# An early load of x, paired scores, and one tile's routing ahead of the other tile's work in a fused eight-mixer kernel

## The reference, cut to what matters

```python
# layer 0: differential attention, 8 heads of 2 maps (16 score maps of head size 64), v of 128
s = einsum('bhmqd,bhmkd->bhmqk', rope(q), rope(k)) * scale       # chunk mask: 64-token chunks
p = softmax(where(mask, s, -inf));  a = p[:, :, 0] - lam * p[:, :, 1]
o = rms_norm(a @ v) * subln_g * (1 - lambda_init)
x = layer_norm(ALPHA * x + o @ w_o)
# PEER, after each attention: 8 heads, 128 keys a side, 16 of 16384 experts a head
scores = einsum('thcd,hckd->thck', (x @ w_pq), sub_keys)
s_top, i_top = top_k(scores, 16)
g_s, g_i = top_k(all 16 x 16 sums of the two sides, 16);  gates = softmax(g_s)
h = gelu(einsum('td,ted->te', x, u[ids]))
ffn = einsum('te,ted->td', gates * h, v[ids])
x = layer_norm(ALPHA * x + ffn)
# layer 1: stick-breaking attention, then PEER again
```

## Time and profile before

| | us |
|---|---|
| median of 3 runs (3049.17 to 3051.73) | 3051.18 |
| the profiled execution | 3059.78 |
| its span, first to last instruction | 3058.1 |
| PE busy (share of the span) | 2584.2 (85%) |
| DVE busy | 1706.0 (56%) |
| ACT busy | 917.5 (30%) |
| POOL busy | 623.6 (20%) |
| mean granted PE clock | 0.961 of 2.4 GHz |

### The profile page before, as it was taken

One profiled execution on the slowest core, in us unless ns is written; L12 is line 12 of the kernel. 1 busy time (PEld: TensorE's weight loads), 2 busy tenths in 40 slices (PEclk: granted clock), 3 DMA queues, 4 the chain that ended last, 5 costly groups with the idle time before them and its releaser, 6 DMA issues.

```text
span 3058.1 us, 29977 instructions
## 1 busy us (share of the span) xinstructions
PE 2584.2 (85%) x10337; PEld 1604.8 (52%) x10337; DVE 1706.0 (56%) x3830; ACT 917.5 (30%) x1906; POOL 623.6 (20%) x623
## 2 busy tenths in 40 slices
PE   7997777777779887777777788999899989998999
PEld 3564222222237562222222245897579767975798
DVE  2336767767641256676776545554455465545654
ACT  1312222222213322222222124442444344423443
POOL 0003444444420023444444302000100000001000
PEclk9888999999999999999999999999999989998999
DMA  7208999999984169999999931553355324543353
GB/s 251 83 21 356 421 421 421 386 422 421 421 329 151 55 233 417 422 421 422 388 421 421 422 133 60 167 190 110 110 165 185 119 83 147 185 147 110 107 183 109
DMA packets 209663, 767.50 MB, mean 251 GB/s; under 512 B 16435, under 2 KB 87686, under 8 KB 143750
## 3 DMA queue, kind: packets, MB, share of 16 engines
q0 software_dynamic: 73760, 536.93, 42.4%
q1 hardware_dynamic: 135782, 229.09, 22.2%
HBM read 764.90 MB, written 1.07 MB: 250 GB/s over the span
## 4 chain that ended last, share of the span: by engine, by line
PE 40%; DMA 6%; DVE 3%; ACT 1%; issue 1%; POOL 0%; DVEq 0%; ACTq 0%; POOLq 0%
PE psum L1161 12%; PE psum L1175 11%; PE psum L917 9%; DMA weights<-in_peer_uv,scratch 4%; PE psum L1123 2%; DMA arena<-in_peer_uv,scratch 2%; PE psum L976 1%; PE psum L904 1%; PE psum L965 1%; PE psum L954 1%; PE psum L950 0%; DVE heads_arena L1939 0%; PE psum L1139 0%; DVE arena L1848 0%; DVE xT L2030 0%
## 5 line engine op out<-in xcount | busy, mean ns | idle before, releaser
L1123 PE MATMUL psum<-weights,scratch 128*128 128x512 f32 x1224 | 576.3, 616 | 202.8 <-ACT scratch L1494 202.8
L1123 PEld LDWEIGHTS psum<-weights,scratch 128*128 128x128 f32 x1224 | 226.0, 193 | 551.8 <-ACT scratch L1494 306.3
L1123 PE MATMUL psum<-arena,scratch 128*128 128x512 f32 x824 | 390.7, 619 | 143.8 <-ACT scratch L1494 143.8
L2333 POOL DMA_INDIRECT weights<-in_peer_uv,scratch x306 | 335.4, 1096 | 643.3 <-PE psum L1123 406.8
L917 PE MATMUL psum<-weights,xT 128*128 128x512 f32 (+2 forms) x1000 | 437.8, 596 | 19.7 <-ACT xT L1337 14.7
L2145 DVE TENSOR_TENSOR piece<-weights,piece 128x2048 fp32r<-128x2048 f32 x128 | 292.8, 2293 | 221.1 <-ACT piece L1535 221.1
L1161 PE MATMUL psum<-split_x,piece 128*128 128x256 f32 x3072 | 386.0, 287 | 5.9 <-DVE split_x L2152 5.9
L1161 PEld LDWEIGHTS psum<-split_x,piece 128*128 128x128 f32 x3072 | 384.0, 196 | 11.4 <-issue 7.4
L1175 PE MATMUL psum<-piece,hidden 128*128 128x512 f32 x1536 | 358.8, 390 | 0.0
L1123 PEld LDWEIGHTS psum<-arena,scratch 128*128 128x128 f32 x824 | 152.7, 195 | 381.0 <-ACT scratch L1494 215.5
L1486 ACT ACTIVATE scratch<-scratch 128x2 f32<-128x2 f32 x256 | 52.0, 203 | 999.0 <-DVE heads_arena L1939 999.0
(11 more groups left out here) (211 smaller groups left out, 2334.1 us busy)
## 6 DMA issues: line engine op xcount, KB each, us to landing
weights<-in_w_up SPq DMA_DIRECT2D x64, 1024.0 KB, 5.5
weights<-in_w_down SPq DMA_DIRECT2D x64, 1024.0 KB, 4.9
weights<-in_w_qkv_a SPq DMA_DIRECT2D x6, 2048.0 KB, 20.0
weights<-in_a_w_in SPq DMA_DIRECT2D x6, 2048.0 KB, 10.5
weights<-in_peer_w_q SPq DMA_DIRECT2D x4, 2048.0 KB, 8.3
weights<-in_w_kv_b SPq DMA_DIRECT2D x4, 2048.0 KB, 12.9
weights<-in_a_w_out SPq DMA_DIRECT2D x4, 2048.0 KB, 7.9
weights<-in_b_w_in SPq DMA_DIRECT2D x3, 2048.0 KB, 10.2
```

The costliest lines, as they stand in the source:

```text
L1123: mm = pe.matmul(psum[g.bank][:, :], diagonal[:, n % DIAGONALS, :], row[:, D + half * BANK:D + (half + 1) * BANK], start=(k == 0), stop=(k ...
L2333: pool.indirect_dma_start(gathered[at % GATHER_SLOTS], None, rows, bass.IndirectOffsetOnAxis(ap=expert[:, t, k:k + 1], axis=0), element_of ...
```

## The change

It touches the start, the differential attention and both PEER stages.

- x and the identity (the first 128 columns of the constants) get a semaphore of their own, and weight chunk 0 is asked for right behind them. PE starts on these; its first projections wait for the copies of their own tile's x.
- q and k are projected first (8 blocks), then v for both tiles' first 512 columns. Tile 0's q and k are transposed, a v block follows, tile 1's transposes, the last v block. `work`, in which DVE rotates, moves to another place in `heads_arena`, in two halves.
- The keys of `diff` are laid out apart (`keys_apart`, eight ACT copies of 64 rows; POOL clears the halves first), and scores are paired. Both tiles are one run of `attend`; the norm's steps move three units later.
- ACT copies tile 0's transposed output before tile 1's square root.
- In both PEER stages PE does tile 0's queries and scores before the last output block of tile 1; DVE routes head 0 before it adds and normalises tile 1, and routes head 1 after it. The queries and scores of tile 1 stand between the first mixes: one chunk before row 0, one after row 1, the scores after row 5.
- The slots get another order, and start at 0 in each layer. Gather 5 waits until tile 1's last output block is projected, gather 8 for tile 1's first query chunk (`groups[1][1]`).

```diff
-            sp.dma_start(x[:, :, :], A["x"][0].rearrange("(t p) d -> p t d", p=P)).then_inc(consts_loaded, 16)
-            sp.dma_start(const[:, :], A["const"]).then_inc(consts_loaded, 16)
+            sp.dma_start(x[:, :, :], A["x"][0].rearrange("(t p) d -> p t d", p=P)).then_inc(x_loaded, 16)
+            sp.dma_start(const[:, 0:P], A["const"][:, 0:P]).then_inc(x_loaded, 16)
+            load_weights(diff_qk, 0, 1)
+            sp.dma_start(const[:, P:], A["const"][:, P:]).then_inc(consts_loaded, 16)
+            load_weights(diff_qk, 1, 2)
...
@@ PE, start and attention @@
-            pe.wait_ge(consts_loaded, CONSTS_LOADED)
-            turns(x_loaded_turn)
-            copied(x_loaded_turn.last)
-            project(diff_in.blocks)
+            pe.wait_ge(x_loaded, X_LOADED)
+            turns(x_loaded_turn)
+            project(diff_qk_blocks[0:1], turned=x_loaded_turn.done[0:2])
+            project(diff_qk_blocks[1:2], turned=x_loaded_turn.done[2:4])
+            project(diff_qk_blocks[2:])
...
+            project(diff_v_blocks[0:2])
             pe.wait_ge(in_ready.sem, diff_turn_in + 1)
-            turns(diff_turn)
-            copied(diff_turn.last)
-            attend(diff, "diff", 0, HEADS)
-            attend(diff, "diff", HEADS, NT * HEADS)
+            turns(diff_turn[0])
+            project(diff_v_blocks[2:3])
+            pe.wait_ge(in_ready.sem, diff_turn_in + 2)
+            turns(diff_turn[1])
+            project(diff_v_blocks[3:4])
+            pe.wait_ge(zeroed.sem, diff_zeroed + 2)
...
+            attend(diff, "diff")
             for t in range(NT):
                 pe.wait_ge(in_ready.sem, diff_out_in + t + 1)
                 turns(diff_out.turn[t])
                 project(diff_out.blocks[t][0:1], turned=diff_out.turn[t].done)
-                if t == NT - 1:
-                    turn_x(peer0, 0, ln_x[0])
-                project(diff_out.blocks[t][1:2])
-            queries(peer0, ln_x[0])
-            for t in range(NT):
-                mix(peer0, t)
+                if t == 0:
+                    project(diff_out.blocks[t][1:2])
+            first_queries(peer0, ln_x[0])
+            project(diff_out.blocks[1][1:2])
+            mixes(peer0, ln_x[0])
...
+            def first_queries(p, x_value):
                 pe.wait_ge(keys_loaded, 32 * (p.layer + 1))
                 turns(p.key_turn)
+                turn_x(p, 0, x_value)
                 copied(p.x_turn[0].last)
+                for n in range(NT):
+                    query_chunk(p.q, 0, n)
                 copied(p.key_turn.last)
                 copied(p.q.groups[0][-1])
                 scores_of(p, 0)
+
+            def mixes(p, x_value):
+                turn_x(p, 1, x_value)
                 copied(p.x_turn[1].last)
+                query_chunk(p.q, 1, 1)
+                mix(p, 0, 0, 2)
+                query_chunk(p.q, 1, 0)
+                mix(p, 0, 2, 6)
+                for g in p.q.groups[1]:
+                    copied(g)
                 scores_of(p, 1)
+                mix(p, 0, 6)
+                mix(p, 1)
...
@@ ACT @@
-            turns(diff_turn)
...
+            diff_values(diff_v_blocks[0:2])
+            diff_turns(0)
+            diff_values(diff_v_blocks[2:3])
+            diff_turns(1)
+            diff_values(diff_v_blocks[3:4])
             exps(diff, None, 0, HEADS + SUBLN_ROOT)
             root(diff_root, PEER_HEADS)
             exps(diff, None, HEADS + SUBLN_ROOT, NT * HEADS)
+            turns(diff_out.turn[0])
             root(diff_root + 1, PEER_HEADS)
-            for t in range(NT):
-                turns(diff_out.turn[t])
+            turns(diff_out.turn[1])
...
                 root(before, 1)
+                turns(p.key_turn)
+                turns(p.x_turn[0])
+                for n in range(2):
+                    queries(0, n)
+                scores_of(0)
                 gate(0, 0)
+                root(before + 1, 1)
+                turns(p.x_turn[1])
                 gate(0, 1)
                 for t in range(NT):
...
+                            if i == 1:
+                                queries(1, 1)
+                            if i == 3:
+                                queries(1, 0)
+                            if i == 5:
+                                scores_of(1)
...
@@ DVE @@
-            def peer(p, ln):
+            def peer(p, out, ln):
+                add_to_x(out.blocks[0], ALPHA)
+                layer_norm(ln - 1, 0)
                 copied(p.s[0][3])
-                for h in range(2):
-                    for _ in route(p, 0, h):
-                        pass
+                for _ in route(p, 0, 0):
+                    pass
+                add_to_x(out.blocks[1], ALPHA)
+                layer_norm(ln - 1, 1)
+                for _ in route(p, 0, 1):
+                    pass
                 shares(p, 0, 0)
                 shares(p, 0, 1)
...
@@ POOL @@
                         if n >= GATHER_SLOTS:
                             pool.wait_ge(value_mixed.sem, p.mixed0 + n - GATHER_SLOTS + 1)
-                        elif at % GATHER_SLOTS == 8:
+                        elif n == OUT_SLOT:
+                            pool.wait_ge(psum_filled[out.blocks[1][1][-1].bank], out.blocks[1][1][-1].filled)
+                        elif n == QUERY_SLOT:
                             pool.wait_ge(psum_filled[p.q.groups[1][1].bank], p.q.groups[1][1].filled)
...
+            for r in range(2):
+                pool.memset(diff_keys[HD * (1 - r):HD * (2 - r), :, r, :], 0.0).then_inc(zeroed.sem, 1)
+                pool.wait_ge(zeroed.sem, diff_zeroed + r + 1)
```

More of the change, by code:

```diff
@@ L210, in build @@
         arena = sb("arena", [P, 8 * D])
-        gathered = [arena[:, n * ROW:(n + 1) * ROW] for n in range(4)]
-        gathered += [weights[:, slot, n * ROW:(n + 1) * ROW] for slot in (2, 3, 1) for n in range(2)]
+        in_arena = [arena[:, n * ROW:(n + 1) * ROW] for n in range(4)]
+        in_slot = {slot: [weights[:, slot, n * ROW:(n + 1) * ROW] for n in range(2)] for slot in (1, 2, 3)}
+        gathered = in_arena[1:4] + in_slot[2] + in_arena[0:1] + in_slot[3] + in_slot[1]
         assert len(gathered) == GATHER_SLOTS
@@ L919, in project, with query_chunk @@
                     mm.then_inc(psum_filled[g.bank], 1)
-            def project_turned(p, t):
-                for c, g in zip(p.chunks, p.groups[t]):
-                    pe.wait_ge(weight_loaded[c.slot], c.loaded)
-                    bank_free(g)
-                    for j in range(SLOT_COLS // P):
-                        for k in range(KB):
-                            mm = pe.matmul(psum[g.bank][:, j * P:(j + 1) * P], c.view[:, k, j * P:(j + 1) * P],
-                                           xT[:, k, t * P:(t + 1) * P], start=(k == 0), stop=(k == KB - 1))
-                    mm.then_inc(psum_filled[g.bank], 1)
+            def query_chunk(p, t, n):
+                c, g = p.chunks[n], p.groups[t][n]
+                pe.wait_ge(weight_loaded[c.slot], c.loaded)
+                bank_free(g)
+                for j in range(SLOT_COLS // P):
+                    for k in range(KB):
+                        mm = pe.matmul(psum[g.bank][:, j * P:(j + 1) * P], c.view[:, k, j * P:(j + 1) * P],
+                                       xT[:, k, t * P:(t + 1) * P], start=(k == 0), stop=(k == KB - 1))
+                mm.then_inc(psum_filled[g.bank], 1)
             def turn_normed(turn, n):
@@ L947, in attend @@
                         g = att.s[i]
-                        if kind not in ("selected", "window"):
+                        if kind == "latent":
                             bank_free(g)
@@ L1112, in scores_of, with mix @@
                     mm.then_inc(psum_filled[g.bank], 1)
-            def mix(p, t):
-                for g in p.mixed[t]:
-                    bank_free(g)
-                for k in range(SEL):
+            def mix(p, t, first=0, last=SEL):
+                if first == 0:
+                    for g in p.mixed[t]:
+                        bank_free(g)
+                for k in range(first, last):
                     n = t * SEL + k
-                    row = gathered[(p.pick0 + n) % GATHER_SLOTS]
+                    row = gathered[p.place(n)[0]]
                     pe.wait_ge(diagonal_ready.sem, p.diagonal0 + n + 1)
@@ L1651, in window @@
                 turns(l.turn[0], None, 0, -1)
-                keys_apart(l.turn[0], 0, 0, KV_HEADS)
+                keys_apart(l.turn[0].groups[-1], 0, 0, KV_HEADS)
                 root(l.root["k1"], KV_HEADS)
@@ L1658, in window @@
                 turns(l.turn[1], None, 0, -1)
-                keys_apart(l.turn[1], 1, 0, KV_HEADS)
+                keys_apart(l.turn[1].groups[-1], 1, 0, KV_HEADS)
             def latent(l):
@@ L2320, in _, with gathers @@
         def _(pool):
-            def gathers(p, t):
+            def gathers(p, out, t):
                 rows = A["peer_uv"].rearrange("l e d -> (l e) d")
@@ L2350, in _ @@
             for t in range(NT):
```

(1 more changed line is left out.)

173 lines of the change are left out of this document (87 added, 86 removed).

## The result

The changed kernel takes 3017.9 us in the median (3017.09 to 3020.8, four runs) against 3051.17 (3049.17 to 3051.73) for the kernel before in the same rounds: a ratio of 0.9894, 95% interval 0.9877 to 0.9911, 33.3 us or 1.1% faster. The prediction was 3024, with a range of 3012 to 3041.

What follows compares the result with a forecast made beforehand. DMA engines were taken to bound the two gather stages, a compute chain the stretches ahead and between. Savings of 11.4 + 1.2 + 11.9 + 6.4 + 0 - 4 = 26.9 us from 3051.18 gave 3024, range 3012 to 3041.

Steps and rivals of the forecast that it cites:

- Start: Start of the program: PE's first projection begins earlier, needing only x, the identity and weight chunk 0; 11.4 us saved.
- Rival C: At the start, weight chunk 0 lands 5 us late behind other packets: 3029 us, chance 0.07.
- the prelude's term: Projections before attention: shorter wait for copies and no DVE wait for the bias rows; 1.2 us saved together.
- Attention: Differential attention: paired scores in one run, tile 1 at full clock with DVE as the bound; 11.9 us saved.
- Rival A: Clock is low in tile 1's attention all the same, attention saving about 0: 3036 us, chance 0.15.
- Output projection: After attention: tile 0's output copy no longer queues behind ACT's square root (4.5), two blocks faster (1.9); 6.4 us saved.
- Ahead of the dots: Opening of each PEER stage: early routing sends the first gather 5.85 us earlier, set against costs moved into the gather stage.
- First layer 0: First PEER layer: the earlier first gather is balanced by the moved load and 2 us idle; 0 us net.
- The load's 5.1 us: First gather stage: loading the next gains and keys, formerly in a free stretch, takes 5.1 us of all DMA engines.
- Second layer -4: Second PEER layer: 5.85 us gained, less 3.1 for the moved load and idle waits of gathers 12 and 16; 4 us lost.
- rival B: PEER stages: load and late slots cost nothing, 5.85 us arrive in each layer; 3014 us, chance 0.08.
- rival D: Opening of both gather stages: PE becomes the bound at 1.2 GHz with the DMA idle; 3084 us, chance 0.04.

Runs made afterwards that it cites:

- late-x kernel: Changed kernel with TensorE's first transpose waiting again for all constants: 3037.04 us against 3019.3 for the unedited changed kernel in the same batch.
- 64-row kernels: Changed kernel with each head's scores a product of its own on 64 rows: 3028.84 us in one attention run, 3037.08 in two runs cut at the tile boundary.
- the undo: Changed kernel with both PEER stages put back in the order of the kernel before: 3022.06 us, ratio 0.9886 to the kernel before.
- seam and 64 rows: Changed kernel with one 64-row score product a head and attention cut in two runs at the tile boundary: 3037.08 us, ratio 0.9953 to the kernel before.

## Why the prediction was right, step by step

**Start.** 11.4 said, 11.0 measured, all of it at the end (the late-x kernel: 19.2 at the first projection, 19.1 at the flip products). Rival C's late chunk did not come: PE waited 1.70 us for it. Where the prelude's term said 1.2, 4.0 arrived up to DVE's first score. Some 3.0 of it are the seven slow products of the kernel before, of which the changed kernel's trace has none: luck of two traces and not the edit, so the term itself is confirmed to about 1 us and no better.

**Attention.** 11.9 said, 14.5 measured from DVE's first score on. The mechanism held: the clock stays, DVE becomes the bound. The size was off in "tile 0 keeps its 0.90 us a unit": from the third to the ninth pair of scores (102.71 to 111.87) it took 0.76, since the 0.90 held the extra 0.34 of a 64-row product. I took it for the columns' price. From DVE's first score to its first of tile 1 (100.66 to 112.93) it is 12.3 us for 14.4 said, most of the 2.6; tile 1 and the end took 26.6 for 27 said. The prediction named both "the seam gone" and "128 rows" for the clock; the runs give the return of the clock to the rows, and leave open what spared it the fall. Rival A (low clock, chance 0.15) is what the 64-row kernels show, at 5.3 us of attention without the seam and 13.4 with it.

**Output projection.** 6.4 said, 6.7 in the traces, 6.9 by undoing it.

**Ahead of the dots.** First gathers 5.85 earlier in each layer: from the end of tile 1's first output block on it is 5.87 in the first layer's traces and 5.85 in the second's (37.66 from 1065.36 on, 31.81 from 1027.98 on), and 5.86 by the undo. First layer 0: right by the undo. Its reasons were half right. The load's 5.1 us hold as far as tested (3.0 for the keys; the gains' part wasn't); "gathers 10 and 11 follow rows 0 and 1" was no limit, since with both behind the pieces nothing changed. Second layer -4: the undo shows +1.7 to -2.4. The step that failed is "gathers 12 and 16 wait for rows 2 and 6: 5.6 + 3.2 us idle". One pause came, 3.5 us, and PE was back at 1.00 for it; rival B (all 5.85 in each layer) and rival D (PE the bound) did not come.

**Sum.** The terms missed by -0.4, +2.8, +2.6, +0.3, +2.6 and +3.8. The stretch between the layers, less its 5.85, took 1.4 more (183.67, 185.11; untouched kernels 183.5 to 185.2), the rest of the program 1.9 less (untouched 1303.4 to 1308.0). Together that is 12.2, the distance from 26.9 to 39.1. By medians the distance is half, 6.1, since before's profiled execution lay 8.6 above its median and after's 2.9. So 3024 is near 3017.9 partly by luck: nearly every term erred the same way, and the distances of the two traced executions from their medians took half of that back.

**Signs of being wrong.** One of the prediction's own came true. The first layer's last gather was to be about 31 us earlier and is 38.8 earlier: about 3 by the slow products of the kernel before, 2.6 by attention, and 2.6 by a gather stage that was shorter than before in the old order too. The second stage moved by 6.0, less than the 8 named. DVE's first score came at 100.66 (near 103 said), the last values ended at 139.5 (near 145), the first gather went out at 194.1 (near 199.5).

**Rivals' prices.** Rival B's 3014 is a slip. If 5.85 arrive in each layer, the terms 0 and -4 both become 5.85, and the kernel takes 3024 - 5.85 - 9.85 = 3008, below the stated range. It did not come, so the slip changed nothing.

## What to carry to other kernels

Put the first operands alone in front and split the wait, and check that what was queued behind is not needed soon: the same wait cost 11 us in one order of loads and 19 in the other. Where a matrix engine works in short products with pauses, fill all rows of the array, even with zeros, before worrying about seams or counts: here it was worth 5 us of 41 without a seam and 13 to 15 with one. In a stage bound by its DMA engines, starting earlier is worth only the idle time that it fills; bytes moved out of it were worth their full time here, and a hole of 6 us closed in it gave 1 to 2 us that can't be told from nothing, so read the last transfer of the stage and not the hole. And before a difference of 3 us between two traces is given to an edit, look whether the first products behind a pause ran at the same rate in both.

## What the runs showed of the hardware

TensorE's clock came back within 4 us from a granted 0.50 to 1.00 under products on 128 rows, and stayed at 0.50 for 28 us under work with 64-row scores (seam and 64 rows, 122 to 150) though PE was busy for 2.00 of every 2 us: a full busy row does not say that the clock will come back. A 64-row score product among 128-row products cost 0.34 us over a 128-row one of the same columns, at clock 1.00 (0.90 against 0.56 us a unit). Behind the first transposes zero to seven projection products ran at 0.85 us instead of 0.43, and where they were slow from the first on the column of the granted clock read 1.00: the steps of the weight loads tell the rate where the column doesn't. The same program gave the same trace to 0.1 us at 842 and at 1714 us on another occasion, while between kernels with different edits an untouched gather stage moved by up to 1.3 us (first layer) and 2.3 us (second). Whether that is the edits ahead of it or plain scatter stays open, since only one kernel was traced twice.
